# Gate and up projections of a two-layer hybrid encoder as seven products for eight over weight tiles, input halves and prompt halves

## What is computed

```python
h2 = rms_norm(x, norm2_g) * (1 + scale2) + shift2
ag = h2 @ w_gate                                   # 1024 -> 2816
ag_c, ffn_conv_new = causal_dwconv(ag, ffn_conv_w, ffn_conv_prev)   # 3 taps over time
y = (jax.nn.silu(ag_c + ffn_conv_b) * (h2 @ w_up)) @ w_down
x = x + gate2 * y
```

## Time and profile before

| | |
|---|---|
| median of 3 runs | 4961.54 us (4959.44 to 4962.13) |
| the profiled execution's own time | 4954.66 us |
| its span | 4952.9 us |
| PE busy, share of the span | 4521.2 us, 91% |
| DVE busy | 1675.3 us, 34% |
| ACT busy | 984.1 us, 20% |
| mean granted TensorE clock | 0.932 of 2.4 GHz |
| feed-forward block up to the down projection, layer 0 | 1448.63 to 2162.80 us |
| the same, layer 1 | 3868.10 to 4555.16 us |

### The profile page before, as it was taken

How to read it: one execution, slowest core, us unless ns; L and a number is a source line. 1 busy time by engine, 2 the same in 40 slices (tenths; PEclk the granted TensorE clock), 3 DMA queues, 4 the chain that set the end, 5 groups by cost and what they waited for, 6 DMA issues and landing times.

```text
span 4952.9 us, 54344 instructions
## 1 busy us (share of the span) xinstructions
PE 4521.2 (91%) x21982; PEld 2516.8 (51%) x21982; DVE 1675.3 (34%) x4031; ACT 984.1 (20%) x1973; POOL 67.8 (1%) x125
## 2 busy tenths in 40 slices
PE   4999888898979999999979998879989899999996
PEld 2545444567545555545535454445675455555553
DVE  2246776435321212110022667663351211111001
ACT  1134543224110000000012344522240100000001
POOL 0000000000000000000000000000000000000000
PEclk8999998688999999999989999977799999999998
DMA  4133112113012222111021111112131011111111
GB/s 168 44 108 132 41 41 81 38 71 117 20 47 74 91 89 77 35 32 35 27 85 57 45 63 46 52 57 73 54 105 48 22 35 35 35 35 33 35 33 44
DMA packets 111290, 292.39 MB, mean 59 GB/s; under 512 B 9280, under 2 KB 57088, under 8 KB 104640
## 3 DMA queue, kind: packets, MB, share of 16 engines
q1 hardware_dynamic: 100816, 243.62, 14.7%
q0 software_dynamic: 9936, 40.58, 2.1%
q10 hardware_dynamic: 288, 4.72, 0.2%
HBM read 243.59 MB, written 45.03 MB: 58 GB/s over the span
## 4 chain that ended last, share of the span: by engine, by line
PE 72%; DVE 10%; issue 10%; DVEq 3%; ACT 2%; PEld 1%; ACTq 1%; SPq 0%; DMA 0%; PEldq 0%; POOL 0%; POOLq 0%
PE PS L735 29%; PE PS L755 12%; PE PS L1254 7%; PE PS L1216 5%; PE PS L1179 2%; DVE big L1631 2%; PE PS L1148 2%; DVE big L1628 2%; DVE hT L1631 2%; PE PS L1185 1%; PE PS L858 1%; DVE big L1766 1%; PE PS L1163 1%; PE PS L691 1%; PE PS L1137 1%
## 5 line engine op out<-in xcount | busy, mean ns | idle before, releaser
L735 PE MATMUL PS<-hT,ring 128*128 128x512 f32 (+1 forms) x4512 | 1476.6, 490 | 95.5 <-DVEq L1677 89.5
L735 PEld LDWEIGHTS PS<-hT,ring 128*128 128x128 f32 x4512 | 746.9, 192 | 823.3 <-issue 733.1
L755 PE MATMUL PS<-hT,ring 128*128 128x512 f32 (+1 forms) x2304 | 859.6, 519 | 0.0
L1254 PE MATMUL PS<-big,ring 128*128 128x512 f32 (+1 forms) x2112 | 683.4, 487 | 3.0 <-DVE big L1631 3.0
L755 PEld LDWEIGHTS PS<-hT,ring 128*128 128x128 f32 x2304 | 376.2, 198 | 323.3 <-issue 311.0
L1254 PEld LDWEIGHTS PS<-big,ring 128*128 128x128 f32 x2112 | 346.4, 191 | 340.0 <-issue 336.6
L1628 DVE SCALAR_TENSOR_TENSOR xT<-PS,mod,xT 128x1024 f32<-128x1024 f32 x32 | 41.1, 1284 | 871.5 <-PE PS L1254 657.6
L1631 DVE TENSOR_TENSOR big<-big,PS 128x512 f32<-128x512 f32 (+2 forms) x200 | 154.4, 795 | 520.8 <-PE PS L735 449.2
L1597 ACT ACTIVATE fext<-PS 128x1024 f32<-128x1024 f32 x44 | 45.1, 1025 | 1118.5 <-PE PS L735 1118.5
L2274 DVE TENSOR_SCALAR big<-fext,par 128x1024 f32<-128x1024 f32 x44 | 35.8, 814 | 655.9 <-ACTq L1599 655.9
L1299 ACT ACTIVATE big<-xT 128x1152 f32<-128x1152 f32 x40 | 46.0, 1161 | 1059.4 <-DVEq L2239 625.2
(11 more groups left out here) (321 smaller groups left out, 3813.2 us busy)
## 6 DMA issues: line engine op xcount, KB each, us to landing
big<-in_w_ada SPq DMA_DIRECT2D x72, 512.0 KB, 5.8
ring<-in_w_in SPq DMA_DIRECT2D x54, 512.0 KB, 3.4
scr<-big POOLq DMA_DIRECT2D x40, 576.0 KB, 3.1
ring<-in_w_gate SPq DMA_DIRECT2D x44, 512.0 KB, 3.6
ring<-in_w_up SPq DMA_DIRECT2D x44, 512.0 KB, 3.7
hT<-in_kcache SPq DMA_DIRECT2D x16, 1024.0 KB, 6.9
hT<-in_vcache SPq DMA_DIRECT2D x16, 1024.0 KB, 7.0
ring<-in_w_down SPq DMA_DIRECT2D x32, 448.0 KB, 3.3
```

The source lines that it names most:

```text
L735: i = mm(pset(n % 2)[:, c0:c0 + m], w[:, k, :], hT[:, k, c0:c0 + m], start=(k == 0), stop=(k == KT - 1))
L755: x = mm(PS[:, o:o + m], w[:, k, :], hT[:, k, c0:c0 + m], start=(k == 0), stop=(k == KT - 1))
L1254: i = mm(pset(m % 2)[:, c0:c0 + n], w[:, k - k0, :], act[:, k * TOK + c0:k * TOK + c0 + n], start=(k == 0), stop=(k == NF - 1))
```

## The change

With the weights of step j as A1 = gate (its first four k), A2 = gate (last four k) and so on, the two weight tiles and the prompt's two halves form a 2 x 2 by 2 x 2 block product. Instead of eight block products of 4 k x 512 columns there are seven, on sums of weight blocks and of input blocks. For this

- DVE makes four sums of the input, once per layer, 2048 columns each (`ft1` to `ft4`; `ft3` in place in `hT`). They lie in `xT`, so ACT issues a copy of `xT` to DRAM (two transfers, `x_mid`) before the norm, and SP loads it back (`x_ret`) in the fifth weight load of the down projection.
- DVE makes four sums of the weights of each step, 512 columns each (`ff_weights`), from both tiles in `ring`.
- PE makes seven products of 4 k x 512 columns (`product`) and the samples' part with the unchanged weights (16 matmuls of 128 columns). Each product has a PSUM bank of its own, and DVE adds them up: five additions before the convolution, two behind it; the closing multiplication is in three pieces.
- Both ring slots of a step are freed when its last product is done. The sums for the next layer's modulation stand ahead of the last product, and use banks 0 and 1.
- Seven semaphores of the gate values of the first mixer are merged to three, with the same waits.

```diff
 def ring_freed(r):
-    return (ff_up if (n - R_FF) % 2 else ff_gate).at(l, j + 1)
+    return ff_prod.at(l, 8 * (j + 1))
 # SP, loads of the down projection
+    if 3 * m + q == 4:
+        sp.wait_ge(*ff_prod.at(l, 8 * NF))
+        sp.wait_ge(*ff_used.at(l, 8 * NF))
+        for k in (0, 4):
+            sp.dma_start(xT[:, k:k + 4, :], x_dram[:, k:k + 4, :]).then_inc(*x_ret.up())
 # PE
+def product(b, w, x):
+    for k in range(4):
+        i = mm(bank(b), w[:, k, :], x[:, k, :], start=(k == 0), stop=(k == 3))
+    i.then_inc(*ff_prod.up())
+def freed(j, n):
+    if j:
+        pe.wait_ge(*ff_used.at(l, 8 * (j - 1) + n))
 for j in range(NF):
-    w = use_w(R_FF + 2 * j)
-    if j:
-        pe.wait_ge(*ff_ext.at(l, j))
-    project(0, w).then_inc(*ff_gate.up())
-    if l == 0:
-        ada_next(j)
-    w = use_w(R_FF + 2 * j + 1)
-    if j:
-        pe.wait_ge(*ff_act.at(l, j))
-    project(1, w).then_inc(*ff_up.up())
+    gate, up = use_w(R_FF + 2 * j), use_w(R_FF + 2 * j + 1)
+    if j:
+        pe.wait_ge(*ff_first.at(l, j))
+    if l == 0 and 4 <= j - 1 < ADA_F + 4:
+        pe.wait_ge(*ada_done.at(0, ADA_P + j))
+    product(0, gate[:, 0:4, :], h_[0][0])
+    freed(j, 2)
+    if l == 0 and 3 <= j - 1 < ADA_F + 3:
+        pe.wait_ge(*ada_rowc.at(0, ADA_P + j + 1))
+    product(1, gate[:, 4:8, :], h_[1][0])
+    freed(j, 8)
+    if j:
+        pe.wait_ge(*ff_smp.at(l, j))
+    for w, o in ((gate, 1024), (up, 1152)):
+        for k in range(KT):
+            i = mm(PS[:, o:o + 128], w[:, k, :], hT[:, k, TPR:TOK], start=(k == 0), stop=(k == KT - 1))
+    i.then_inc(*ff_prod.up())
+    if j == 0:
+        pe.wait_ge(*ff_sums.at(l, 1))
+    pe.wait_ge(*ff_pre.at(l, j + 1))
+    for b, used, w, x in ((3, 1, fs2, ft2), (4, 7, fs1, ft1), (5, 4, fs3, ft3), (6, 5, fs4, h_[1][1])):
+        freed(j, used)
+        product(b, w, x)
+    if l == 0:
+        ada_next(j)
+    freed(j, 6)
+    product(7, up[:, 4:8, :], ft4)
 # ACT
+for i in range(2):
+    sc.wait_ge(*wout_added.at(l, 4 * i + 4))
+    k = 4 - 4 * i
+    sc.dma_start(x_dram[:, k:k + 4, :], xT[:, k:k + 4, :]).then_inc(*x_mid.up())
 norm(l, 1)
 # DVE, before step 0
+dv.wait_ge(*x_mid.at(l, 2))
+tt_(ft1, h_[0][1], h_[0][0], ALU.subtract)
+dr()
+tt_(ft2, h_[1][1], ft1, ALU.subtract)
+tt_(ft3, h_[1][1], h_[0][1], ALU.subtract)
+dr()
+tt_(ft4, ft2, h_[1][0], ALU.subtract)
+dr().then_inc(*ff_sums.up())
+ff_weights(0)
+def ff_weights(j):
+    # waits for both weight tiles of step j and for product 7 of step j - 1's eight
+    tt_(fs1, a2[:, 0], a2[:, 1], ALU.add)
+    tt_(fs3, a1[:, 0], a2[:, 0], ALU.subtract)
+    dr()
+    tt_(fs2, fs1, a1[:, 0], ALU.subtract)
+    dr()
+    tt_(fs4, a1[:, 1], fs2, ALU.subtract)
+    dr().then_inc(*ff_pre.up())
 def ff(j, p, jj):
     ff_prep(j)
-    dv.wait_ge(*ff_ext.at(l, j + 1))
+    # fext = the sum of the products of its half; each step waits for its own product
+    tt_(fu, first, bank(3), ALU.add).then_inc(*ff_used.up())
+    tt_(first, first, bank(1), ALU.add).then_inc(*ff_used.up())
+    tt_(second, fu, bank(4), ALU.add).then_inc(*ff_used.up())
+    tt_(fu, fu, bank(5), ALU.add).then_inc(*ff_used.up())
+    tt_(second, second, bank(6), ALU.add).then_inc(*ff_used.up())
...
     dr().then_inc(*ff_tail.up())
+    if j + 1 < NF:
+        ff_weights(j + 1)
+    if l == 0:
+        ada_next(j)
+    dv.wait_ge(*ff_prod.at(l, 8 * j + 8))
+    tt_(fv, fu, bank(7), ALU.subtract).then_inc(*ff_used.up())
+    tt_(fu, fu, bank(4), ALU.add).then_inc(*ff_used.up())
+    dr()
     dv.wait_ge(*ff_silu.at(l, j + 1))
-    dv.wait_ge(*ff_up.at(l, j + 1))
-    tt_(aj, aj, pset(1), ALU.mult).then_inc(*ff_act.up())
+    tt_(aj[:, 0:512], aj[:, 0:512], fv, ALU.mult)
+    tt_(aj[:, 512:1024], aj[:, 512:1024], fu, ALU.mult)
+    tt_(aj[:, TPR:TOK], aj[:, TPR:TOK], PS[:, 1152:1280], ALU.mult)
+    dr().then_inc(*ff_used.up())
```

More of the change, by code:

```diff
@@ L298, in build @@
         fstate_in = signal("fstate_in", 1, 16)
-        ff_gate = signal("ff_gate", NF)
-        ff_ext = signal("ff_ext", NF)
+        x_mid = signal("x_mid", 2, 16)
+        x_ret = signal("x_ret", 2, 16)
+        ff_sums = signal("ff_sums", 1)
+        ff_pre = signal("ff_pre", NF)
+        ff_prod = signal("ff_prod", 8 * NF)
+        ff_used = signal("ff_used", 8 * NF)
+        ff_first = signal("ff_first", NF)
+        ff_smp = signal("ff_smp", NF)
         ff_conv = signal("ff_conv", NF)
         ff_silu = signal("ff_silu", NF)
-        ff_up = signal("ff_up", NF)
-        ff_act = signal("ff_act", NF)
         ff_tail = signal("ff_tail", NF, 1, 1)
@@ L395, in build @@
         stat = big[:, o_cs2 + 1024:o_cs2 + 1048]
+        h_ = [[hT[:, 4 * k:4 * k + 4, 512 * c:512 * c + 512] for c in range(2)] for k in range(2)]
+        ft1, ft2, ft4 = [xw_[:, i * 2048:(i + 1) * 2048].rearrange("p (k t) -> p k t", k=4) for i in range(3)]
+        ft3 = h_[0][1]
+        fs1, fs2, fs3, fs4 = [xw_[:, 6144 + i * 512:6656 + i * 512].rearrange("p (k c) -> p k c", k=4) for i in range(4)]
+        fu, fv = xw_[:, 8192:8704], xw_[:, 8704:9216]
         HALF = (slice(0, 64), slice(64, 128))
@@ L699, in ada_turn @@
                     pe.wait_ge(*ada_done.at(0, n))
-                mm(PS[:, 3584:3620], (modrow if n < 4 + ADA_P else modrow_f)[n % 2], sel36, start=True, stop=True).then_inc(*ada_cols.up())
+                mm(PS[:, o:o + 36], (modrow if n < 4 + ADA_P else modrow_f)[n % 2], sel36, start=True, stop=True).then_inc(*ada_cols.up())
             for i in range(4):
@@ L1631, in tt_, with ada_copy @@
                 return V.tensor_tensor(out, in0, in1, op)
-            def ada_copy(n):
+            def ada_copy(n, o=3072):
                 dv.wait_ge(*ada_rows.at(0, n + 1))
@@ L2230, in residual @@
                     dv.wait_ge(*done.at(l, pos + 1))
-                    if c == 0:
-                        dv.wait_ge(*x_back.at(l, 2))
+                    if pos == 0:
+                        dv.wait_ge(*(x_ret if c else x_back).at(l, 2))
                     ps = pset(pos % 2)
@@ L2261, in ff_prep @@
                     V.tensor_copy(fes[:, :, 0:2], act[:, bass.ds((NF - 1) * TOK + j * 16, 16)].rearrange("p (b x) -> p b x", b=NB))
+                def ff_weights(j):
+                    for n in range(2):
+                        r = l * R_ALL + R_FF + 2 * j + n
+                        dv.wait_ge(w_loaded[r % 4].sem, 16 * (r // 4 + 1))
+                    r = l * R_ALL + R_FF + 2 * j
+                    a1, a2 = [ring[:, (r + n) % 4, :].rearrange("p (h k c) -> p h k c", h=2, k=4) for n in range(2)]
+                    if j:
+                        dv.wait_ge(*ff_prod.at(l, 8 * (j - 1) + 7))
+                    tt_(fs1, a2[:, 0], a2[:, 1], ALU.add)
[14 more added lines that the diff above has]
+                ff_weights(0)
                 def ff(j, p, jj):
                     aj = act[:, j * TOK:j * TOK + TOK]
+                    first, second = fext[:, 2:514], fext[:, 514:1026]
                     if j == 12:
@@ L2292, in ada_next @@
                             dv.wait_ge(*par_next_in.at(0, 1))
-                        ada_place(ADA_P + j, mod_next, 4 * (j - 4), par_next)
+                        ada_place(ADA_P + j, mod_next, 4 * (j - 4), par_next, o=0)
                     if 3 <= j < ADA_F + 3:
-                        ada_copy(ADA_P + j + 1)
+                        ada_copy(ADA_P + j + 1, o=512)
                 if l == 0:
```

75 lines of the change are left out of this document (40 added, 35 removed).

## The result

The changed kernel takes 5035.3 us (median of 4 runs, 5031.1 to 5041.2) against 4961.8 us of the kernel before on the same chip: a ratio of 1.015, 95% interval 1.0134 to 1.0166. It is 1.5% slower, 73.5 us.

What follows compares the result with a forecast made beforehand. PE's matmul time was taken as the bound. Layer 1's block -41.5, layer 0's +84.6 and small parts +1.0 gave +44 us: 5005.5 us from 4961.5, with a range of 4966 to 5035.

Steps and rivals of the forecast that it cites:

- Removed from PE: Matmul columns of a feed-forward step: 18432 down to 16384, 27.6 us, 3.45 less; at most 151.7 us over 44 steps.
- DVE's loop: Feed-forward steps: PE waits 1.35 us for DVE ahead of the samples, so a plain step takes 28.95 us, not 27.6.
- plain steps: Feed-forward steps of both layers without modulation sums: forecast at 28.95 us each, 2.1 less than before.
- Layer 0, steps 4 to 13: Feed-forward steps with modulation sums: PE idles 10.1 us for late weights and placing, clock loss 2.3; 42.1 us against 33.32.
- Steps 3, 14 and 15: Layer 0's feed-forward steps next to those ten: forecast at 38.75, 33.25 and 35.55 us.
- The blocks in sum: Feed-forward blocks of both layers: layer 0 forecast at +84.6 us, layer 1 at -41.5 us.
- The small parts: Outside the blocks: ACT's spill issue before the norms +1.0 us; spill and load back hidden, merged semaphores nothing.
- Sum: Whole kernel: -41.5 + 84.6 + 1.0 = +44 us, to 5005.5 us.
- DVE's loop fits: Rival, chance 0.07: the 29 plain steps take 27.6 us, 39 us less, 4966 us, no change.
- Weight loads not hidden before: Rival, chance 0.02, on PE: eight fewer exposed weight loads per step, 38 us off, 4967 us.
- The weights come in time: Rival, chance 0.07: SP's loads in layer 0's steps 4 to 14 land before DVE asks; 4909 us, faster.
- The clock stays low for longer: Rival, chance 0.07, in the blocks: longer low clock, or DVE's loop 1 us longer; 29 + 12 us on top, 5045.

Runs made afterwards that it cites:

- e3: Changed kernel with DVE's weight sums for the next step moved behind the closing multiplications: 4939.2 us, ratio 0.9967 to the kernel before.
- e6: Kernel before with only the spill of x, its load back and the merged gate semaphores, without the products: 4973.8 us, ratio 1.0041.
- e7: Kernel before with five unused matmuls (4.3 us) ahead of layer 0's down projection: 4973.8 us, ratio 1.0032.
- e1: Changed kernel with each step's weight loads issued ahead of the modulation transfers: 4950.4 us, ratio 0.9988 to the kernel before.
- e4: Changed kernel with loads ahead of modulation transfers, weight sums behind the multiplications, placing ahead of the tail copies: 4836.0 us, ratio 0.9761 to the kernel before.
- e8: Kernel before with two unused matmuls (1.7 us) ahead of layer 0's down projection: 4956.6 us, ratio 1.0004.
- e5: Changed kernel with ten unused matmuls put behind product 7 in steps 4 to 13 of layer 0: 5009.1 us, ratio 1.0113 to the kernel before.

## Why the prediction was wrong

The sign, and the mechanism and the places in the two blocks, were right; the size was not: +73.5 us for +44, 0.3 us above the range. In the profiled executions it is +81.9 for +44. About half of the miss lies in the blocks, in terms that were sized too small, and half in a stage that the sum had at nothing. Term by term:

- **Removed from PE.** 27.6 us of work a step: e3 has 27.61. The samples alone in line cost nothing more, and 88 records with 88 loads take the time of their columns. The rule of the Trainium skill (TensorE: Matmul & The Clock Gate, Part 3: Packing small matmuls, The mechanism), by which a load overlaps running matmuls only when its row group differs, did not show in these 27.61 us.
- **DVE's loop.** 28.95 forecast, 29.25 measured in most plain steps. The chain was right in kind and 0.3 us short in length; over the 29 plain steps, six of which took 29.6, that is 10 us. The idle of 1.37 us is the forecast's 1.35. The rest lies around it: from the start of the first two products to that of the samples are 8.40 us here and 6.87 in e3, 0.16 more than the idle, and from there to the next product 3.68 us for 3.57.
- **Layer 0, steps 4 to 13.** 42.1 forecast; the starts of the first product go from 1577.42 to 2003.58 us in ten steps, 42.6 each. The idle is 9.6 to 11.1 us for 10.1; the weights have landed 10.0 to 11.0 us after the sums, 10.5 in the mean, for 10.3. The clock loss is 2.4 us in the mean (9.48 - 7.03) for 2.3, so the lower bound of 0 was wrong. The reading of the earlier trace rows was a little off (the two shares put the end of the half clock 4.3 us behind the start, not 3.9), but no term used it. The twenty middle slices of the flow have 395 GB/s in the mean, 18 of them over 358: the 358 GB/s by which the Trainium skill (DMA: Bandwidth & Descriptors, Where 436 GB/s comes from) bounds loads from HBM did not bind.
- **Steps 3, 14 and 15.** Counted as the forecast does, from the end of the product into bank 6 to that of the next step, step 14 took 36.4 us for 33.25: behind 3.42 us of idle the two products took 9.93 us. The forecast had no clock loss there, although it had 2.3 us of loss behind the 5.4 us of step 15 (35.3 measured for 35.55). Step 3 took 39.9 us for 38.75.
- **The blocks in sum.** With the clock loss of the down projections, which the forecast had in the blocks' ends, they are +95.4 for +84.6 and -33.5 for -41.5: 19 us of the miss. The plain steps have 10 of it, steps 4 to 13 some 4, steps 3 and 14 together 4; the others nearly cancel.
- **The small parts.** +1.0 forecast for the norms, +2.5 measured; e6 shows it as the spill's issue in front of the norm and half-clock matmuls behind it.
- **The step that failed.** The sum took every other stage as it was ("The small parts" and "Sum"): it had the mixer of layer 1 at no change, without a row for it. That stage has the same instructions and took 18.6 us more, all of it in PE's busy time (+19.0) at a lower granted share. e7 shows that a delay of 4.4 us alone does this for 14 of them. The changed kernel has the same pattern in the same place: its value matmuls too have 6.4 us of the 18.6. The other orders of it give 8.7 to 18.5 us, and its own moment of arrival was not shifted alone, so why it is 18.6 here and not 8.7 stays open. The forecast had a rival for a longer low clock, but inside the blocks.

The time lies so close to the range that any of these terms, sized rightly, would have brought it inside. That would not have made the working right: half of the miss came from a stage that it had at nothing.

The rivals: "DVE's loop fits" and "Weight loads not hidden before" fall with the rows of the result (29.25 us a plain step) and e3 (27.61). "The weights come in time" did not happen, but e1 made it happen, and at close to its price: 79.5 us for the 97 worked out, with 3.4 us of idle left in each step for `ada_place`. "The clock stays low for longer", 5045, was the nearest in time, 10 us off, and that by luck: behind the idles of the blocks, where it had its loss, the clock cost 2.4 us for 2.3; the longer low clock was in the mixer.

## What to carry to other kernels

Fewer columns on the busiest engine are worth what the orders of the other queues let through: here 151.7 us of matmuls were taken out, and three waits, none of them due to a lack of DMA or DVE time, made the two blocks 195 us longer than they are in e4, with the waits taken out. When a step is moved, look at what its completion releases in an in-order queue (SP loaded the next weights only behind transfers that wait for these sums), and at the piece of work that can go behind the signal which the bottleneck engine waits for. And where a kernel runs PE with gaps, a change of 0.3% (e7) can come from its timing alone: compare the untouched stages before reading a small difference as the edit's.

## What the runs showed of the hardware

- Times of this kernel, whose PE has gaps, do not add up: 4.4 us more of work gave +16 us, 1.8 us more gave none that can be told (e7, e8). The difference is matmul time at a lower granted share (0.87 for 0.89 in the mixer of layer 1). Runs of one program (e8, and the kernel before) fall into groups some 9 and 17 us above the lowest.
- A little more idle was followed by a loss of over four times its length. Behind 3.26 us the 48 records of the norm took 15.78 us, behind 3.64 us 17.47; and behind 3.42 us two products took 9.93 for 7.03. The length of the idle alone does not decide: in e5 2.47 us cost 1.7 us and 2.96 us nothing. This is the row of the changed kernel's norm:

```profile
1408.47 17.47 PE L727 MATMUL PS<-big,cf 128*128 128x512 f32 x48 [3.64 <-ACT big L1335]
```

- Unused matmuls in a gap can pay: with 100 of them (of 512 columns) in e5 the ratio is 1.0113 where it was 1.015, and the profiled span 23.5 us shorter, 14.7 of them in the block where they stand.
